# Adding the attention masks by a matrix product in place of a masked reduction

## The chip, the cores and the metric

The kernel runs on one core of a Trainium2 chip. The metric is the device time of one execution in microseconds (us); of several executions the median is given. A core has TensorE (PE in the rows, its weight loads as PEld), VectorE (DVE), ScalarE (ACT), GpSimd (POOL) and SyncE (SP), which run side by side and wait for each other by semaphores.

## The reference

One sequence of 256 positions with 1024 channels goes through four layers and their norms, all in 32-bit numbers: a layer of attention in a sliding window with a sink ("a", 16 heads), a layer of causal attention ("b", 16 heads), and two hybrid layers ("h", 8 heads each) with dilated attention, a state-space scan and a gated feed-forward part. Every attention has this core; the mask differs per kind:

```python
s = jnp.einsum('bnikgd,bnjkd->bnkgij', qb, kband).astype(jnp.float32) * scale
...
s = jnp.where(mask[None, :, None, None], s, NEG)
sink = jnp.broadcast_to(sinks.astype(jnp.float32).reshape(kvh, G)[None, None, :, :, None, None],
                        s.shape[:-1] + (1,))
p = jax.nn.softmax(jnp.concatenate([s, sink], axis=-1), axis=-1)[..., :-1]
o = jnp.einsum('bnkgij,bnjkd->bnikgd', p.astype(v.dtype), vband)
```

A softmax needs the greatest masked score of each row. A head has 64 channels, and scale is 1/8.

## The kernel before, in words

Nearly all work is projections: 512-column products of activations with weight chunks (L1000). A 32-bit weight chunk comes by DMA into `raw`; ScalarE rounds it to `hi` (L1161), VectorE takes the rest as `lo` (L901), each in two halves, and TensorE multiplies hi and lo parts, three products for one. There are three buffers of each, and a half is split two chunks ahead of its use (`due`).

Everything else is a list of steps that `build_schedule` writes down in one order; every engine walks through this list and issues its own part of each step, so the order on each engine is fixed by the list. `attention(sc, n)` places the attention of one pair of heads beside the projection chunks: first `pv` of the pair before last, then `flip` of the last pair, then `scores` of the new pair. Between two such calls stand the twelve products of half a chunk, and in some places more.

A 128-row query tile by its keys gives 128 columns for the first tile and 256 for the second; the 384 columns of a head (`QC`) lie side by side in one PSUM bank. A step `scores` does this for two heads:

- TensorE (L1040 to L1056) waits until both banks are free, and multiplies queries by keys, 64 rows deep, one head on rows 0 to 63, the other on rows 64 to 127 (L1052 for the first query tile, L1055 for the second).
- VectorE (L1639 to L1648), for each head and each of the two tiles, runs one `tensor_tensor_reduce`: it adds the mask to the scores, scales by -1/8, writes the result back into the bank, and puts the minimum (in "a" begun from the negated sink, else from `BIG`) into `shift`, one number per row and tile. The mask is in `masks`, bf16, three strips of 384 columns with 0 or -1e30. The profile shows each as two instructions of L1644.
- ScalarE (L1285 to L1295) takes the exponential of minus the bank plus `shift` into `prob` (L1293, L1294).

`flip` transposes `prob` (three products of 128 columns a head, L975), ScalarE copies the result out (L1301; in "h" VectorE multiplies, L1654), `pv` multiplies by the values (L1075 to L1077), and `oev` copies the output out of PSUM on ScalarE (L1308). Steps other than projections take PSUM banks 4 to 7 in turn; a bank is free when the last reader of its former content is done. `identb`, the identity in bf16, is made at the start for the `decay` steps of the scan, which add their own mask by products (L1129, L1132).

Of the kernel before, what the change touches and what calls it, by code (L numbers as in the profile page):

```python
# [26 lines left out]
ALU = mybir.AluOpType  # L27
ACT = mybir.ActivationFunctionType
AXX = mybir.AxisListType.X

S, D, P = 256, 1024, 128
# [1 line left out]
KD = D // P  # L33
HD = 64
NEG = -1e30
BIG = 3e38
EPS = 1e-5
SCALE = HD ** -0.5
FF = 2816
# [15 lines left out]
QC = 3 * P  # L55
# [637 lines left out]
def build(nc, t):  # L693
# [24 lines left out]
    def keep(name, shape, dt=F32):  # L718
        return at(name, shape, dt)[0]

    at.end = 0
    h = keep("h", [P, M, D])
# [8 lines left out]
    masks = keep("masks", [P, 3 * QC + P + 32], BF16)  # L731
    csum = keep("csum", [P, P], BF16)
    identb = keep("identb", [P, P], BF16)
# [10 lines left out]
    sinks = keep("sinks", [P, 2, 16])  # L744
    small = keep("small", [P, 2, 3, 16])
    taps = keep("taps", [P, 10 * NCT])
    convw = taps[:, 0:8 * NCT].rearrange("p (l t c) -> p l t c", l=2, t=4)
    convb = taps[:, 8 * NCT:10 * NCT].rearrange("p (l c) -> p l c", l=2)
    shift = keep("shift", [P, 16, M])
    esink = keep("esink", [P, 16, M])  # L750
    dens = keep("dens", [P, M, 8])
# [89 lines left out]
    psum = [nc.alloc_psum_tensor(f"bank{i}", [P, 512], F32) for i in range(8)]  # L841
# [27 lines left out]
    def freed(eng, bank):  # L869

        if bank.before is not None:
            step, who = bank.before.freed
            if step.kind == "flip":
                eng.wait_ge(sem["flip", who], step.n + 1)
            else:
                ended(eng, step, who)
        return psum[4 + bank.at]
# [95 lines left out]
    def _(pe):  # L973
# [4 lines left out]
        for s in sc.steps:  # L978
# [61 lines left out]
            elif s.kind == "scores":  # L1040
# [6 lines left out]
                ended(pe, a["tq"][hd // 4], "scalar")  # L1047
                bank = freed(pe, s.bank)
                both = (bank, freed(pe, s.pair.bank))
                q, k = B["qT"], B["kT"]  # L1050
                for r, bank in zip((0, 64), both):
                    nc.tensor.matmul(bank[:, 0:P], q[r:r + 64, hd // 2, 0:P], k[r:r + 64, kv, 0:P],  # L1052
                                     start=True, stop=True)
                for r, bank in zip((0, 64), both):
                    nc.tensor.matmul(bank[:, P:QC], q[r:r + 64, hd // 2, P:S], k[r:r + 64, kv, 0:S],  # L1055
                                     start=True, stop=True).then_inc(sem["scores", "tensor"], 1)  # L1056
            elif s.kind == "flip":
                a = s.att
                B = Hb if a["kind"] == "h" else A
# [91 lines left out]
    def _(act):  # L1151
# [12 lines left out]
        def done(ins, s):  # L1164
            ins.then_inc(sem[s.kind, "scalar"], 1)
# [23 lines left out]
        for s in sc.steps:  # L1189
# [95 lines left out]
            elif s.kind == "scores":  # L1285
# [3 lines left out]
                if s.i >= 2:  # L1289

                    act.wait_ge(sem["flip", "tensor"], s.i - 1)
                bank, pr = psum[4 + s.bank.at], B[f"prob{s.p % 2}"]
                nc.scalar.activation(pr[:, 0:P], bank[:, 0:P], ACT.Exp, scale=-1.0, bias=shift[:, hd, 0:1])  # L1293
                done(nc.scalar.activation(pr[:, P:QC], bank[:, P:QC], ACT.Exp, scale=-1.0,  # L1294
                                          bias=shift[:, hd, 1:2]), s)  # L1295
            elif s.kind == "flip" and s.att["kind"] != "h":
                act.wait_ge(sem["flip", "tensor"], s.i + 1)
# [159 lines left out]
    def _(dve):  # L1457
        tt, ts, stt = nc.vector.tensor_tensor, nc.vector.tensor_scalar, nc.vector.scalar_tensor_tensor

        def chained(ins):  # L1460
            link(dve, "vector", ins)
# [5 lines left out]
        def done(ins, s):  # L1467
            ins.then_inc(sem[s.kind, "vector"], 1)
# [70 lines left out]
        for s in sc.steps:  # L1539
# [99 lines left out]
            elif s.kind == "scores":  # L1639
                a, hd = s.att, s.head  # L1640
                dve.wait_ge(sem["scores", "tensor"], s.i + 1)
                bank, at_ = psum[4 + s.bank.at], {"a": 0, "b": 1, "h": 2}[a["kind"]] * QC
                for m, c in enumerate((slice(0, P), slice(P, QC))):
                    last = nc.vector.tensor_tensor_reduce(  # L1644
                        bank[:, c], bank[:, c], masks[:, at_ + c.start:at_ + c.stop], -SCALE,
                        sinks[:, 1, hd:hd + 1] if a["kind"] == "a" else BIG, ALU.add, ALU.min,
                        shift[:, hd, m:m + 1])
                done(last, s)  # L1648
            elif s.kind == "flip" and s.att["kind"] == "h":
                dve.wait_ge(sem["flip", "tensor"], s.i + 1)  # L1650
                if s.i >= 2:
# [163 lines left out]
```

## Time and profile before

| | us |
|---|---|
| median of 3 runs | 922.65 |
| lowest, highest | 921.39, 923.07 |
| profiled execution, its own time | 923.07 |
| its span in the trace | 921.2 |
| TensorE busy | 882.9 |
| VectorE busy | 558.5 |
| ScalarE busy | 518.6 |
| GpSimd busy | 127.7 |

The span runs from the first to the last instruction of the program; the execution's time lies around it. Busy times of engines overlap. A product's busy time includes its way through the array, so two products that follow each other overlap in the rows; their starts tell the pace.

### The profile page before, as it was taken

The numbers are of one execution on the slowest core, as the hardware profiler recorded it, in microseconds if no ns is written. First come the engines' busy times: TensorE is split into PE (matmuls) and PEld (weight loads), VectorE is DVE, ScalarE is ACT, GpSimd is POOL, SyncE is SP. The second block draws the span as 40 slices with busy tenths as digits, with TensorE's granted clock in tenths as the row PEclk, the third lists the DMA queues.
The fourth block names the chain that finished last, engine by engine and source line by source line (L and its number), as shares of the span: only waits on it lengthen the run. The fifth ranks groups of instructions, "written<-read, shape, count | busy, mean of one in ns | idle before, by whom it ended". The sixth has DMA issues, their size and how long they took to land.

```text
span 921.2 us, 12293 instructions
## 1 busy us (share of the span) xinstructions
PE 882.9 (96%) x4557; PEld 728.8 (79%) x4557; DVE 558.5 (61%) x969; ACT 518.6 (56%) x853; POOL 127.7 (14%) x103
## 2 busy tenths in 40 slices
PE   4899998999999999999999999999999999999995
PEld 3787887878787888788888888887888888888884
DVE  4754578546766567865555544756677755555443
ACT  3567755676487685464444433677874644444331
POOL 0031103421015350000000000042430000000000
PEclk9899999999999999999999999999999999999998
DMA  8641344443544424576565555534423766565521
GB/s 279 218 150 57 129 163 157 140 129 102 177 167 139 137 93 136 164 236 187 188 185 183 183 183 185 193 104 139 137 92 120 246 190 188 186 190 189 196 95 46
DMA packets 94846, 146.88 MB, mean 159 GB/s; under 512 B 6476, under 2 KB 54852, under 8 KB 94788
## 3 DMA queue, kind: packets, MB, share of 16 engines
q1 hardware_dynamic: 91392, 139.14, 46.3%
q0 software_dynamic: 1440, 5.24, 2.0%
q10 hardware_dynamic: 1956, 1.71, 0.5%
q8 instruction: 37, 0.61, 0.3%
q14 instruction: 21, 0.17, 0.1%
HBM read 145.04 MB, written 1.05 MB: 159 GB/s over the span
## 4 chain that ended last, share of the span: by engine, by line
PE 70%; issue 21%; DVE 3%; ACT 2%; DMA 2%; POOL 0%; ACTq 0%; POOLq 0%; DVEq 0%
PE bank L1000 55%; PE bank L975 6%; PE bank L1141 1%; PE bank L1052 1%; PE bank L1055 1%; PE bank L1077 1%; PE bank L1076 1%; DMA taps_stage<-in_conv_b 1%; PE bank L1075 1%; DMA gains<-in_norm_g 1%; ACT junk L1186 1%; DVE lo L901 1%; ACT hi L1161 1%; DVE hyb_MT L1749 1%; PE bank L1120 0%
## 5 line engine op out<-in xcount | busy, mean ns | idle before, releaser
L901 DVE TENSOR_TENSOR lo<-raw,hi 128x1024 fp32r<-128x1024 f32 x246 | 302.4, 1254 | 133.7 <-ACT hi L1161 131.6
L1161 ACT ACTIVATE hi<-raw 128x1024 fp32r<-128x1024 f32 x262 | 268.4, 1056 | 77.0 <-PE bank L1000 69.9
L1000 PE MATMUL bank<-hi,xT_hi 128*128 128x512 f32 (+2 forms) x736 | 294.4, 400 | 8.5 <-DVE lo L901 3.1
L1000 PE MATMUL bank<-hi,xT_lo 128*128 128x512 f32 (+2 forms) x736 | 285.5, 388 | 0.0
L1000 PE MATMUL bank<-lo,xT_hi 128*128 128x512 f32 (+2 forms) x736 | 284.5, 387 | 0.0
L1000 PEld LDWEIGHTS bank<-hi,xT_hi 128*128 128x128 f32 x736 | 140.0, 190 | 41.6 <-issue 13.8
L1000 PEld LDWEIGHTS bank<-hi,xT_lo 128*128 128x128 f32 x736 | 139.6, 190 | 28.9
L1000 PEld LDWEIGHTS bank<-lo,xT_hi 128*128 128x128 f32 x736 | 140.3, 191 | 25.5 <-issue 0.5
L1000 PE MATMUL bank<-hi,hT 128*128 128x512 f32 x352 | 111.2, 395 | 0.0
L1000 PEld LDWEIGHTS bank<-hi,hT 128*128 128x128 f32 x352 | 66.3, 188 | 15.4
L1000 PE MATMUL bank<-lo,hT 128*128 128x512 f32 x176 | 69.4, 395 | 0.0
L1000 PE MATMUL bank<-hi,oT_hi 128*128 128x512 f32 x160 | 66.9, 418 | 0.0
L1000 PE MATMUL bank<-hi,oT_lo 128*128 128x512 f32 x160 | 62.7, 392 | 0.0
L1000 PE MATMUL bank<-lo,oT_hi 128*128 128x512 f32 x160 | 62.4, 390 | 0.0
L1208 ACT ACTIVATE hT<-bank 128x512 fp32r<-128x512 f32 x22 | 13.2, 598 | 77.2 <-PE bank L975 77.2
L1577 DVE TENSOR_TENSOR hT<-bank,hT 128x512 fp32r<-128x512 f32 x22 | 15.2, 692 | 59.3 <-ACT hT L1208 59.3
L975 PE MATMUL bank<-cst,quarter 128*128 128x128 f32 x264 | 39.4, 277 | 12.0 <-DVE quarter L1571 10.1
L1258 ACT ACTIVATE silu_gate<-bank,rms 128x256 f32<-128x256 f32 x44 | 20.7, 475 | 50.3 <-PE bank L1000 50.3
L975 PEld LDWEIGHTS bank<-cst,quarter 128*128 128x128 f32 x264 | 32.8, 143 | 20.2 <-issue 10.3
L901 POOL TENSOR_TENSOR lo<-raw,hi 128x1024 fp32r<-128x1024 f32 x16 | 38.2, 2399 | 74.1 <-ACT hi L1161 74.1
L1612 DVE SCALAR_TENSOR_TENSOR quarter<-bank,rms,silu_gate 128x256 f32<-128x256 f32 x44 | 19.3, 479 | 41.1 <-ACT silu_gate L1258 41.1
L1736 DVE SCALAR_TENSOR_TENSOR hyb_acc<-bank,taps,hyb_acc 128x255 f32<-128x255 f32 (+2 forms) x72 | 29.2, 474 | 19.9 <-ACT hyb_acc L1333 19.9
(230 smaller groups left out, 983.5 us busy)
## 6 DMA issues: line engine op xcount, KB each, us to landing
raw<-in_w_in SPq DMA_DIRECT2D x26, 1024.0 KB, 5.1
raw<-in_w_gate SPq DMA_DIRECT2D x44, 512.0 KB, 4.0
raw<-in_w_up SPq DMA_DIRECT2D x44, 512.0 KB, 4.9
raw<-in_w_down SPq DMA_DIRECT2D x22, 1024.0 KB, 4.9
raw<-in_w_out SPq DMA_DIRECT2D x20, 1024.0 KB, 5.1
raw<-in_w_in_b SPq DMA_DIRECT2D x10, 1024.0 KB, 5.1
raw<-in_w_in_a SPq DMA_DIRECT2D x8, 1024.0 KB, 7.8
gains<-in_norm_g POOLq DMA_DIRECT2D x2, 512.0 KB, 6.8
```

The costliest lines, as they stand in the source:

```text
L901: return engine.tensor_tensor(lo[r][:, cols], raw[c.i % RAW][:, cols], hi[r][:, cols].bitcast(F32), ALU.subtract)
L975: return nc.tensor.transpose(out, in_, ident)
L1000: last = nc.tensor.matmul(bank[:, 0:wd], still[a], mv[r][:, off:off + wd], start=c.first and i == 0 and j == 0, stop=c.last and i == len(t ...
L1052: nc.tensor.matmul(bank[:, 0:P], q[r:r + 64, hd // 2, 0:P], k[r:r + 64, kv, 0:P], start=True, stop=True)
L1055: nc.tensor.matmul(bank[:, P:QC], q[r:r + 64, hd // 2, P:S], k[r:r + 64, kv, 0:S], start=True, stop=True).then_inc(sem["scores", "tensor"], 1)
L1075: nc.tensor.matmul(bank[:, c0:c0 + W1], pt[:, 0:P], v[:, 0, kv, :], start=True, stop=True)
L1161: nc.scalar.activation(hi[c.i % SPLIT][:, cols], raw[c.i % RAW][:, cols], ACT.Copy)\
L1208: done(nc.scalar.activation(out, bank[:, :], ACT.Copy), s)
L1258: last = nc.scalar.activation(sil[s.i % 2][:, m, :], bank[:, 0:UPW], ACT.Silu, scale=rms[:, 1, m:m + 1])
L1577: done(tt(b, bank[:, :], a.bitcast(F32), ALU.subtract), s)
L1612: last = stt(quarter[s.buf][:, m * UPW:(m + 1) * UPW], psum[2 * s.block["pair"] + m][:, UPW:2 * UPW], rms[:, 1, m:m + 1], sil[s.i % 2][:, ...
L1736: ins = stt(acc[:, tap:S], x[:, 0:S - tap], cw[:, 3 - tap, ct:ct + 1], acc[:, tap:S], ALU.mult, ALU.add)
```

## The change

The mask is put into the banks by TensorE: before the score products, and after the waits for the banks, each of the two banks gets one product of `identb` with the mask's strip of 384 columns, which starts the accumulation; the score products then add to it. VectorE takes the plain maximum of the 128 and the 256 columns into a new tile `rowmax` (L1647, L1648 of the changed kernel), waits for its own second maximum, and makes `shift` of both by one operation on 128x2 elements: times -1/8, in "a" also the minimum with the negated sink. The bank is not written by VectorE any more, and ScalarE's exponential uses the scale 1/8 in place of -1.

```diff
-BIG = 3e38
...
+    rowmax = keep("rowmax", [P, 2, 4])
...
                 both = (bank, freed(pe, s.pair.bank))
+                mk = {"a": 0, "b": 1, "h": 2}[a["kind"]]
+                for bank in both:
+                    nc.tensor.matmul(bank[:, 0:QC], identb[:, :], masks[:, mk * QC:(mk + 1) * QC],
+                                     start=True, stop=False)
                 q, k = B["qT"], B["kT"]
                 for r, bank in zip((0, 64), both):
                     nc.tensor.matmul(bank[:, 0:P], q[r:r + 64, hd // 2, 0:P], k[r:r + 64, kv, 0:P],
-                                     start=True, stop=True)
+                                     start=False, stop=False)
                 for r, bank in zip((0, 64), both):
                     nc.tensor.matmul(bank[:, P:QC], q[r:r + 64, hd // 2, P:S], k[r:r + 64, kv, 0:S],
-                                     start=True, stop=True).then_inc(sem["scores", "tensor"], 1)
+                                     start=False, stop=True).then_inc(sem["scores", "tensor"], 1)
...
-                nc.scalar.activation(pr[:, 0:P], bank[:, 0:P], ACT.Exp, scale=-1.0, bias=shift[:, hd, 0:1])
-                done(nc.scalar.activation(pr[:, P:QC], bank[:, P:QC], ACT.Exp, scale=-1.0,
+                nc.scalar.activation(pr[:, 0:P], bank[:, 0:P], ACT.Exp, scale=SCALE, bias=shift[:, hd, 0:1])
+                done(nc.scalar.activation(pr[:, P:QC], bank[:, P:QC], ACT.Exp, scale=SCALE,
                                           bias=shift[:, hd, 1:2]), s)
...
                 dve.wait_ge(sem["scores", "tensor"], s.i + 1)
-                bank, at_ = psum[4 + s.bank.at], {"a": 0, "b": 1, "h": 2}[a["kind"]] * QC
-                for m, c in enumerate((slice(0, P), slice(P, QC))):
-                    last = nc.vector.tensor_tensor_reduce(
-                        bank[:, c], bank[:, c], masks[:, at_ + c.start:at_ + c.stop], -SCALE,
-                        sinks[:, 1, hd:hd + 1] if a["kind"] == "a" else BIG, ALU.add, ALU.min,
-                        shift[:, hd, m:m + 1])
-                done(last, s)
+                rm = rowmax[:, s.i % 2, :]
+                nc.vector.tensor_reduce(rm[:, 0:1], psum[4 + s.bank.at][:, 0:P], AXX, ALU.max)
+                chained(nc.vector.tensor_reduce(rm[:, 1:2], psum[4 + s.bank.at][:, P:QC], AXX, ALU.max))
+                if a["kind"] == "a":
+                    done(ts(shift[:, hd, :], rm[:, 0:2], -SCALE, sinks[:, 1, hd:hd + 1], ALU.mult, ALU.min), s)
+                else:
+                    done(ts(shift[:, hd, :], rm[:, 0:2], -SCALE, None, ALU.mult), s)
```

On TensorE, at the first pair of heads of the first layer, stood before (an x2 is the pair's two heads; hi and lo are the weight parts, bank is a PSUM bank):

```order
L1000 MATMUL bank<-lo_61,xT_hi 128x512
L1000 MATMUL bank<-hi_58,xT_lo 128x512
L1052 MATMUL bank<-attn_kT,attn_qT 128x128 x2
L1055 MATMUL bank<-attn_kT,attn_qT 128x256 x2
L1000 MATMUL bank<-hi_59,xT_hi 128x512
L1000 MATMUL bank<-lo_62,xT_hi 128x512
```

and now:

```order
L1000 MATMUL bank<-lo_61,xT_hi 128x512
L1000 MATMUL bank<-hi_58,xT_lo 128x512
L1052 MATMUL bank<-masks,identb 128x384 x2
L1056 MATMUL bank<-attn_kT,attn_qT 128x128 x2
L1059 MATMUL bank<-attn_kT,attn_qT 128x256 x2
L1000 MATMUL bank<-hi_59,xT_hi 128x512
L1000 MATMUL bank<-lo_62,xT_hi 128x512
```

The row of `masks` is new, two products; the score products keep their place behind it, and nothing else of TensorE's order moves.

On VectorE, for the same pair, stood before (ISA is the masked reduction and, with 128x1, the read of its result; the waits are the ones for TensorE's scores and for ScalarE's half of a split):

```order
L901 TENSOR_TENSOR lo_60<-raw_54,hi_57 128x1024 [waits chunk_scalar] x2
L1644 ISA bank,shift<-bank,masks,sinks 128x128 [waits scores_tensor]
L1644 ISA shift 128x1
L1644 ISA bank,shift<-bank,masks,sinks 128x256
L1644 ISA shift 128x1
L1644 ISA bank,shift<-bank,masks,sinks 128x128 [waits scores_tensor]
L1644 ISA shift 128x1
L1644 ISA bank,shift<-bank,masks,sinks 128x256
L1644 ISA shift 128x1
L901 TENSOR_TENSOR lo_61<-raw_55,hi_58 128x1024 [waits chunk_scalar]
```

and now:

```order
L901 TENSOR_TENSOR lo_60<-raw_54,hi_57 128x1024 [waits chunk_scalar] x2
L1647 TENSOR_REDUCE rowmax<-bank 128x1 [waits scores_tensor]
L1648 TENSOR_REDUCE rowmax<-bank 128x1
L1650 TENSOR_SCALAR shift<-rowmax,sinks 128x2 [waits chain_vector]
L1647 TENSOR_REDUCE rowmax<-bank 128x1 [waits scores_tensor]
L1648 TENSOR_REDUCE rowmax<-bank 128x1
L1650 TENSOR_SCALAR shift<-rowmax,sinks 128x2 [waits chain_vector]
L901 TENSOR_TENSOR lo_61<-raw_55,hi_58 128x1024 [waits chunk_scalar]
```

Eight instructions of a pair became six; the last of each head waits for the one before it, and behind it in the queue stand the second head's maxima and the next split.

## Rows read from the trace of the kernel before

**Rows 1.** The page's busy times, and a stretch of attention: us, busy, ..., PEclk, DMA share, GB/s

```profile
PE 882.9 (96%) x4557; PEld 728.8 (79%) x4557; DVE 558.5 (61%) x969; ACT 518.6 (56%) x853; POOL 127.7 (14%) x103
...
50.00:110.00 60.00, 58.70 (x370) 48.33 (x370) 30.70 (x85) 44.19 (x85) 14.70 (x13) 1.00 0.30 100
```

**Rows 2.** Waits of TensorE: line <- releaser: us in total, times, longest

```profile
PE bank L1052 <- ACT hyb_o L1308: 2.7, 2, 1.4
PE bank L1052 <- ACT attn_o L1308: 2.5, 2, 1.3
```

**Rows 3.** L1052's records (ns), then timeline 52 to 60: start, us, engine, line [idle]

```profile
L1052 PE MATMUL bank<-attn_kT,attn_qT x64: 272/308/374, 53.8 to 208.9; 64*128 64x128 f32 x64
...
53.23 0.39 PE L1000 MATMUL bank<-lo,xT_hi 128*128 128x512 f32 x1
...
53.45 0.39 PE L1000 MATMUL bank<-hi,xT_lo 128*128 128x512 f32 x1
53.77 0.30 PEld L1052 LDWEIGHTS bank<-attn_kT,attn_qT 64*128 64x128 f32 x4 [0.35 <-issue]
...
56.53 0.47 ACT L1294 ACTIVATE attn_prob<-bank,shift 128x256 f32<-128x256 f32 x1
...
57.49 0.81 PE L975 MATMUL bank<-cst,attn_prob 128*128 128x128 f32 x6
...
58.24 0.30 PEld L1052 LDWEIGHTS bank<-attn_kT,attn_qT 64*128 64x128 f32 x4 [0.17 <-issue]
```

**Rows 4.** L1129's weight loads (ns), then the critical chain: start, us, what

```profile
L1129 PEld LDWEIGHTS bank<-masks,identb x64: 96/98/99, 327.9 to 696.9; 128*128 128x128 bf16 x64
...
328.09 0.06 PE bank L1132
...
328.92 0.06 PE bank L1132
```

**Rows 5.** VectorE's timeline at one pair of the first layer and one of the second

```profile
71.62 0.36 DVE L1644 CUSTOM_DVE_ANT_0 bank<-bank,masks,sinks 128x128 f32<-128x128 f32 x1 [2.16 <-PE bank L1055]
...
72.30 0.14 DVE L1644 DVE_READ_ACCUMULATOR2_ANT shift<- 128x1 f32 x1
...
72.98 0.14 DVE L1644 DVE_READ_ACCUMULATOR2_ANT shift<- 128x1 f32 x1
...
185.34 0.30 DVE L1644 CUSTOM_DVE_ANT_0 bank<-bank,masks 128x128 f32<-128x128 f32 x1 [2.28 <-PE bank L1055]
...
185.56 0.47 DVE L1644 CUSTOM_DVE_ANT_0 bank<-bank,masks 128x256 f32<-128x256 f32 x1
...
186.57 0.14 DVE L1644 DVE_READ_ACCUMULATOR2_ANT shift<- 128x1 f32 x1
```

**Rows 6.** VectorE's timeline at the chained Newton steps of the first norm

```profile
27.57 0.17 DVE L1597 TENSOR_SCALAR newt<-newt 128x2 f32<-128x2 f32 x1
27.78 0.16 DVE L1598 TENSOR_TENSOR rms<-rms,newt 128x2 f32<-128x2 f32 x1
27.86 2.35 DVE L901 TENSOR_TENSOR lo<-raw,hi 128x1024 fp32r<-128x1024 f32 x2
```

**Rows 7.** Timelines of ScalarE and TensorE before two waits for L1308

```profile
72.48 0.37 ACT L1293 ACTIVATE attn_prob<-bank,shift 128x128 f32<-128x128 f32 x1 [1.16 <-DVE shift L1644]
...
77.30 0.39 ACT L1308 ACTIVATE attn_o<-bank 128x260 f32<-128x260 f32 x1
...
77.84 0.49 PE L1052 MATMUL bank<-attn_kT,attn_qT 64*128 64x128 f32 x4 [1.30 <-ACT attn_o L1308]
...
288.44 0.37 ACT L1293 ACTIVATE hyb_prob<-bank,shift 128x128 f32<-128x128 f32 x1 [2.05 <-DVE shift L1644]
...
296.51 0.36 ACT L1308 ACTIVATE hyb_o<-bank 128x260 f32<-128x260 f32 x1
```

**Rows 8.** The page's group of VectorE's splits: busy us, mean ns, idle before

```profile
L901 DVE TENSOR_TENSOR lo<-raw,hi 128x1024 fp32r<-128x1024 f32 x246 | 302.4, 1254 | 133.7 <-ACT hi L1161 131.6
```

**Rows 9.** A group of VectorE by line: busy us, mean ns, idle before

```profile
L1749 DVE TENSOR_TENSOR hyb_MT<-hyb_E,hyb_cb 128x512 f32<-128x512 f32 x16 | 14.0, 887 | 4.0 <-ACT hyb_E L1366 4.0
```

## The prediction

> **What bounds the kernel now.** I read the page's busy times first, then the table of waits of TensorE, then the timeline around the score products, and last the timelines of VectorE and ScalarE there. TensorE is busy for 882.9 of 921.2 us [rows 1]; the chain that ended last runs mostly through it. So whatever is added to TensorE's stream is paid unless it falls into a wait, and whatever is taken from VectorE pays only where TensorE waits for it. The reader should see in the waits that TensorE's whole waiting at the score products is 2.7 + 2.5 = 5.2 us, at four places, and that there it waits for ScalarE (L1308, the copy of the attention output out of PSUM) [rows 2].
>
> There are 16 + 16 + 8 + 8 = 48 heads, taken two at a time, so 24 pairs. A product of 32-bit operands leaves two records; 64 records for the first two layers [rows 3] are 32 heads.
>
> **The added matrix products.** Each pair gets two products of the identity with a mask strip, bf16, 384 columns, all 128 rows of the array: 48 in all. None has this width in the trace. The nearest rows are L1129 and L1132, bf16 products of 128 columns, which follow each other in 0.06 us: from 328.09 to 328.92 there are 14 steps, 0.059 us each [rows 4]. Three times that is 0.177 us, an upper end, since whatever is fixed in a product is counted three times. The granted clock in attention is 1.00, the 2.4 GHz level [rows 1], so 0.059 us are 142 clocks for 128 columns; at exactly a clock a column 384 columns would take 0.160 us, the lower end. The 512-column products of the projections start 0.22 us apart (53.23, 53.45) [rows 3]; three quarters of that is 0.165 us, and I take that, as the nearest row in width: 48 x 0.165 = 7.9 us, with ends 48 x 0.160 = 7.7 and 48 x 0.177 = 8.5 us. The weight load of such a product takes 0.10 us [rows 4], and the 128-column products keep a step of 0.059 us although each has one, so it lies beside the product before it.
>
> Does the change of array shape cost anything new? The score products use half the rows (64*128). Their first weight load comes 0.32 us after the start of the last projection product (53.45 to 53.77), which another projection product would have followed after 0.22 us; and after the flips, whose six products step by 0.11 us, the last one starts at 57.49 + 0.81 - 0.27 = 58.03 and the load at 58.24, 0.21 us later [rows 3]. So entering the half-row shape costs about 0.10 us beyond the step of the product in front, whichever it is. With the change the mask product stands in front; the number of switches stays. It costs nothing more where TensorE runs without a wait. The Trainium skill (TensorEngine Tiling (Array Packing), Key Properties) says that changing the tiling mode drains the engine; the rows agree with about 0.10 us of it, and by that rule alone the sum would be the same, as the masks sit on the 128-row side of a switch that was there before.
>
> At the four places where TensorE waits before the scores, the 0.10 us used to pass inside the wait. Now the masks come after the wait (the wait is for the bank they write) and the switch after them: 4 x 0.10 = 0.4 us more.
>
> **VectorE's part of a pair.** Removed: 96 masked reductions and their 96 accumulator reads of 0.14 us, and the writing of the masked scores back into the bank. Added: 96 plain maxima, 48 waits of VectorE for its own maximum, and 48 operations on 128x2 elements. Before, a pair in the first layer took 1.50 us (71.62 to 72.98 + 0.14), and the first head's numbers were there at 72.30 + 0.14 = 72.44. In the later layers, where the limit is a constant, a pair took 1.37 us (185.34 to 186.57 + 0.14); there the second reduction starts 0.22 us after the first and takes 0.47 us [rows 5]. No plain maximum stands in the trace. It has one operand fewer and writes no strip back. If it costs what the masked one does, with the steps of the later layers, a head is 0.22 + 0.47 (the second must now end) + 0.03 + 0.17 = 0.89 us, and the next head starts some 0.09 us before that end: 0.80 + 0.89 = 1.69 us a pair against 1.37. The 0.03 us and the 0.17 us are read from the Newton steps, which are chained in the same way (27.57, 0.17 long, next at 27.78), and the 0.09 us from the unchained successor at 27.86 of the step at 27.78 [rows 6]. If it is 0.1 us shorter each, the pair takes about 1.4 us, as now. So the latency of the pair changes by 0 to +0.35 us, and I take +0.25, nearer the row of the same width and source, because the wait for the end is certain and the saving is not.
>
> Where does this lie on the path? At most pairs nowhere. After the scores of the first pair TensorE has twelve projection products; ScalarE's last exponential ends at 56.53 + 0.47 = 57.00 and the flips start at 57.49 [rows 3], the second head's 0.33 us later, so the head that is late has 0.8 us of slack; and the table of waits names no wait of a flip (L975) for ScalarE at any pair. VectorE's next split (L901) is queued behind the new wait, but VectorE stands idle before its splits for 131.6 us in all, waiting for ScalarE [rows 8]. But the four waits of 1.3 us are another matter: there ScalarE runs without a pause from the first exponential (72.48, which waited for VectorE) over the second head's, the split, a table load and the gate's silu to the copy L1308 at 77.30, and TensorE starts the next scores at 77.84 after 1.30 us of waiting. The same chain runs in the hybrid layers from 288.44 to 296.51 [rows 7]. What VectorE is late there, TensorE pays one to one: 4 x 0.25 = 1.0 us, ends 0 and 4 x 0.35 = 1.4 us.
>
> ScalarE's 96 exponentials keep their count and size; only a constant and what stands in the bank change: nothing. Memory traffic: none.
>
> **Sum.** 7.9 + 0.4 + 1.0 = 9.3 us on TensorE's path. The profiled execution took 923.07 us (span 921.2), so it would be 932.4; it lay 0.42 us above the median of 922.65, so the median becomes 932.0 us (+1.0%). Ends: 7.7 + 0.4 + 0 = 8.1 and 8.5 + 0.4 + 1.4 = 10.3 us, that is 930.7 and 933.0.
>
> **Rivals.**
> (1) *Slow maxima.* VectorE could take far longer over a plain maximum. The dearest row per column is L1749, 887 ns for 512 columns, 1.73 ns a column [rows 9]; at that rate, with the 0.17 us of a 128x2 operation as fixed part, the two of a head take 0.39 and 0.61 us, the second starting 0.31 us after the first; a head takes 0.31 + 0.61 + 0.20 = 1.12 us, a pair 2.15 us, +0.8. On the four chains this is 3.2 us, and two or three tight pairs begin to wait (0.4 us together): 7.9 + 0.4 + 3.2 + 0.4 = 11.9 us, 934.6. Against it: the masked reduction of 256 columns takes 0.47 us, two operands and all. Chance 0.08. The Trainium skill (VectorE: DVE Perf Modes, Rules for kernel authors) calls tensor_reduce the slowest VectorE operation and advises to restructure; it speaks against this change, and no row here shows a reduction of that kind.
> (2) *Masks that do not stream.* If every mask product must be out of the array before what follows it (the first for the change of number type, the second because it follows one), each costs 0.165 + 0.10 us: 48 x 0.265 = 12.7, and with 0.4 + 1.0 us as above 14.1 us, 936.8. For it: 0.10 us is what a switch does cost here. Against it: L1132 adds into the columns that L1129 has just written at a step of 0.059 us. Chance 0.06.
> (3) *Cheap all round.* Masks at a clock a column, and maxima so short that the first exponential starts 0.3 us earlier and the four waits shrink by as much: 7.7 + 0.4 - 1.2 = 6.9 us, 929.6. Chance 0.08.
> (4) *Faster.* If a mask product were bound by issue and not by its columns, it would cost the 0.06 us of L1129: 2.8 us. If VectorE's stage then shrank by over 1 us a pair, the waits before the scores, 5.2 us, would go: 2.8 - 5.2 = -2.4 us, 920.3. It decides below (5.2 - 1.8) / 48 = 0.07 us a mask, and only with all four waits gone. Against it: TensorE's steps follow the columns (0.059 us for 128, 0.22 for 512), and the new VectorE stage has one more dependent step. Chance 0.02; with half of it, no change, 0.02.
>
> **How the numbers follow.** Forecast 0.74, (1) 0.08, (2) 0.06, (3) 0.08, (4) 0.02, no change 0.02. A measurement of this kernel can tell about 0.2% (1.8 us) from none. Slower by more than that: 0.74 + 0.08 + 0.06 + 0.08 = 0.96; same 0.02; faster 0.02. The range takes in the forecast's ends and some 1 us on either side for the spread of the runs (921.39 to 923.07 before), up to the edges of (3) and (1): 929.8 to 934.2.
>
> **What the changed profile should show.** 48 more bf16 products before the half-row ones, 0.16 to 0.18 us apart; TensorE's busy time up by about 8 us; from the last 512-column product to the first score weight load 0.22 + 0.165 + 0.165 + 0.10 = 0.65 us in place of 0.32. The maxima with their 128x2 step should take 1.6 to 1.8 us a pair in place of 1.37 to 1.50, and the four waits before the scores should grow from 5.2 to about 6.2 us. Outside attention nothing moves. I am wrong if the masks step by under 0.1 us or over 0.2 us, if those waits shrink, or if the flips begin to wait for ScalarE.

## The result, and the profile after

The changed kernel takes 933.76 us (median of 4 runs, 932.42 to 935.81), the kernel before, measured beside it, 922.02 us (4 runs, 920.93 to 923.07). The ratio is 1.0137, with an interval from 1.0116 to 1.0158: slower by 11.7 us, where 9.3 us were forecast. The upper end of the forecast's range, 934.2, lies 11.55 us above the 922.65 us it was worked out from; the distance measured here is just beyond it. The profiled execution took 933.77 us, its span is 932.0 us.

The page of the changed kernel, busy times, against 882.9 us of TensorE before [rows 1]:

```profile
PE 891.8 (96%) x4605; PEld 731.1 (78%) x4605; DVE 565.8 (61%) x921; ACT 520.2 (56%) x853; POOL 127.4 (14%) x103
```

TensorE's table of waits in the changed kernel (line that waited, engine and line it waited for, us in total, times, longest), cut to the rows that answer to [rows 2] or are new:

```profile
PE bank L1052 <- ACT hyb_o L1312: 3.1, 2, 1.6
PE bank L1052 <- ACT attn_o L1312: 2.9, 2, 1.5
...
PE bank L1087 <- DVE hyb_probT L1658: 1.0, 1, 1.0
...
PE bank L1052 <- DVE hyb_acc L1740: 0.2, 1, 0.2
```

The four waits grew from 5.2 to 6.0 us, as forecast (6.2). Two waits are new: 1.0 us before L1087, the sums of the scan in the first hybrid layer, and 0.2 us before the masks of a later pair there.

The new instructions, from the views of the lines L1052, L1647, L1648, L1650 and L1652 (duration in ns as least, median and greatest; then first and last start in us; then the shape):

```profile
L1052 PE MATMUL bank<-masks,identb x48: 322/323/337, 51.6 to 643.3; 128*128 128x384 bf16 x48
```

```profile
L1647 DVE TENSOR_REDUCE rowmax<-bank x48: 274/285/293, 53.0 to 645.3; 128x1 f32<-128x128 f32 x48
```

```profile
L1648 DVE TENSOR_REDUCE rowmax<-bank x48: 406/414/418, 53.2 to 645.5; 128x1 f32<-128x256 f32 x48
```

```profile
L1650 DVE TENSOR_SCALAR shift<-rowmax,sinks x16: 228/229/810, 53.6 to 98.7; 128x2 f32<-128x2 f32 x16
```

```profile
L1652 DVE TENSOR_SCALAR shift<-rowmax x32: 168/169/821, 170.8 to 645.9; 128x2 f32<-128x2 f32 x32
```

The plain maximum of 256 columns takes 0.41 us, less than the masked one of 0.47 [rows 5], and nowhere near the 0.61 of rival (1). What stands out is the third column of the last two rows: the operation on 128x2 elements sometimes takes 0.8 us in place of 0.17.

TensorE's timeline at the first two pairs of the first layer (start and duration in us; an x2 or x4 is a run of products under its first start):

```profile
51.37 0.39 PE L1000 MATMUL bank<-hi,xT_lo 128*128 128x512 f32 x1
51.60 0.50 PE L1052 MATMUL bank<-masks,identb 128*128 128x384 bf16 x2
52.03 0.49 PE L1056 MATMUL bank<-attn_kT,attn_qT 64*128 64x128 f32 x4
```

```profile
55.74 0.82 PE L975 MATMUL bank<-cst,attn_prob 128*128 128x128 f32 x6
56.39 0.49 PE L1052 MATMUL bank<-masks,identb 128*128 128x384 bf16 x2
```

The last projection product starts at 51.37, the masks at 51.60, the scores at 52.03: 0.66 us in place of the 0.32 of [rows 3], and 0.65 was forecast. The masks step by 0.165 us (the x2 runs 0.50 us, one product 0.32 to 0.34) and the switch of shape takes the rest of the 0.43 us. Behind the flips of the second pair, whose last starts at 55.74 + 0.82 - 0.27 = 56.29, the masks come 0.10 to 0.11 us later, which is the flips' own step.

At the third pair this is no longer so. The timelines of TensorE and ScalarE in the changed kernel:

```profile
61.84 0.82 PE L975 MATMUL bank<-cst,attn_prob 128*128 128x128 f32 x6
62.58 0.48 PE L1052 MATMUL bank<-masks,identb 128*128 128x384 bf16 x2
```

```profile
62.04 0.39 ACT L1312 ACTIVATE attn_o<-bank 128x260 f32<-128x260 f32 x1 [0.61 <-PE bank L1081]
```

and the same place in the kernel before:

```profile
63.28 0.82 PE L975 MATMUL bank<-cst,attn_prob 128*128 128x128 f32 x6
64.03 0.49 PE L1052 MATMUL bank<-attn_kT,attn_qT 64*128 64x128 f32 x4
```

```profile
63.48 0.39 ACT L1308 ACTIVATE attn_o<-bank 128x260 f32<-128x260 f32 x1 [0.53 <-PE bank L1077]
```

In both, ScalarE's copy of the output out of PSUM, which frees one of the two banks, ends while the flips still run, at 62.04 + 0.39 = 62.43 and at 63.87, and TensorE starts in the bank 0.15 and 0.16 us after that. Before, this lay inside the 0.20 us that lead from the last flip to a half-row product anyway: at the second pair, where no bank is waited for, it is 0.20 us too [rows 3]. Now the masks could follow the last flip after 0.11 us, and come after 0.19 (62.39 to 62.58). At 0.08 us such a gap is too short to be a wait in the table. The place with a long wait shows the same 0.14 us between the end of the copy, 76.83 + 0.39 = 77.22, and the masks:

```profile
76.83 0.39 ACT L1312 ACTIVATE attn_o<-bank 128x260 f32<-128x260 f32 x1
```

```profile
77.36 0.48 PE L1052 MATMUL bank<-masks,identb 128*128 128x384 bf16 x2 [1.53 <-ACT attn_o L1312]
```

VectorE's part of the first pair in the changed kernel:

```profile
52.98 0.29 DVE L1647 TENSOR_REDUCE rowmax<-bank 128x1 f32<-128x128 f32 x1 [1.14 <-PE bank L1059]
53.19 0.41 DVE L1648 TENSOR_REDUCE rowmax<-bank 128x1 f32<-128x256 f32 x1
53.64 0.29 DVE L1650 TENSOR_SCALAR shift<-rowmax,sinks 128x2 f32<-128x2 f32 x1
...
54.48 0.23 DVE L1650 TENSOR_SCALAR shift<-rowmax,sinks 128x2 f32<-128x2 f32 x1
```

From 52.98 to 54.71 it takes 1.73 us (1.50 before [rows 5]), in the later layers about 1.55 (1.37 before).

The new wait of 1.0 us has its cause some microseconds ahead of it. VectorE, GpSimd and TensorE in the changed kernel, three views of the same stretch:

```profile
280.90 2.50 DVE L1713 TENSOR_TENSOR hyb_da<-hyb_dt,small 128x48 f32<-128x48 f32 x2
283.33 1.01 DVE L1658 TENSOR_TENSOR hyb_probT<-bank,cst 128x384 f32<-128x384 f32 x2
```

```profile
280.98 4.69 POOL L901 TENSOR_TENSOR lo<-raw,hi 128x1024 fp32r<-128x1024 f32 x2 [5.04 <-ACT hi L1165]
```

```profile
284.02 0.38 PE L1087 MATMUL bank<-hyb_da,cst 128*128 128x32 f32 x2 [0.96 <-DVE hyb_probT L1658]
```

and VectorE and GpSimd in the kernel before:

```profile
276.18 0.33 DVE L1709 TENSOR_TENSOR hyb_da<-hyb_dt,small 128x48 f32<-128x48 f32 x2
```

```profile
276.30 4.80 POOL L901 TENSOR_TENSOR lo<-raw,hi 128x1024 fp32r<-128x1024 f32 x2 [4.86 <-ACT hi L1161]
```

Two small operations of VectorE, which write `hyb_da`, took 0.33 us before and take 2.50 us now. Nothing in them changed. Before, GpSimd started a split 0.12 us after the first of the two, which is just when the second started, and neither was held; now it starts 0.08 us after the first, and the second operation, 0.04 us later than GpSimd, ends only when GpSimd's first half (4.69 / 2 = 2.35 us) is over. `hyb_probT`, queued behind it, is late, and so are the sums on TensorE. The second hybrid layer shows the same collision (the pair of operations takes 2.53 us at 619.73), but there `hyb_probT` had waited 1.98 us for TensorE's flips before, which covers it.

### The profile page after: what moved, and what is told of

Same layout as the page of the kernel before. It is cut to its first block, busy times and chain, and to the rows that moved or that the text cites. A ratio compares the mean times of both kernels' runs of the same rounds, so it can differ in the third digit from the quotient of the medians.

```text
span 932.0 us, 12341 instructions
## 1 busy us (share of the span) xinstructions
PE 891.8 (96%) x4605; PEld 731.1 (78%) x4605; DVE 565.8 (61%) x921; ACT 520.2 (56%) x853; POOL 127.4 (14%) x103
## 4 chain that ended last, share of the span: by engine, by line
PE 66%; issue 21%; DVE 6%; ACT 4%; DMA 2%; POOL 0%; ACTq 0%; POOLq 0%; DVEq 0%
PE bank L1000 51%; PE bank L975 6%; DVE lo L901 1%; PE bank L1145 1%; PE bank L1059 1%; DMA taps_stage<-in_conv_b 1%; PE bank L1056 1%; PE bank L1081 1%; PE bank L1080 1%; ACT hi L1165 1%; PE bank L1052 1%; ACT junk L1190 1%; PE bank L1079 1%; DMA gains<-in_norm_g 1%; DVE hyb_MT L1753 1%
## 5 line engine op out<-in xcount | busy, mean ns | idle before, releaser
L975 PE MATMUL bank<-cst,quarter 128*128 128x128 f32 x264 | 39.4, 277 | 11.7 <-DVE quarter L1575 9.8
```

The costliest lines, as they stand in the source:

```text
L975: return nc.tensor.transpose(out, in_, ident)
```

## The experiments

The median of the kernel before was 921.26 us in the first group of runs, 919.93 in the second and 919.99 in the third; each ratio is against the one of its own group. "Step" below is what one pair of heads adds on TensorE's path: how much further the first projection product behind its scores has moved against the kernel before, since the same point of the pair ahead. Steps leave out what lies ahead of the first pair, where the change does nothing: there the profiled execution of the kernel before, at a granted clock of 0.93 in its first 51 us, was 2.8 us later than that of the repeated change, at 0.97.

**The change once more**, beside the others of the first group, the kernel unaltered.

> The changed kernel once more, on the same chip as the parts: 11 to 12 us over before. The sum of the parts is 9 + 1 = 10 by theory F, and more than the parts if the arrival and the longer VectorE stage collide only together.

Measured: 931.82 us, ratio 1.0115 (1.0096 to 1.0133). The steps add up to 11.3 us: 0.32 or 0.33 at most of the pairs that open a layer (two each), 0.36 to 0.42 at most others, 0.59 at the four waited ones, 1.31 at the pair with the late sums. That is more than the medians differ by (10.6 us) and less than in the first measurement (11.7).

**Masks by product alone.** The products are added, VectorE keeps its masked reduction (so the mask is in the scores twice).

```diff
 # before.py
+                for bank in both:
+                    nc.tensor.matmul(bank[:, 0:QC], identb[:, :], masks[:, mk * QC:(mk + 1) * QC],
+                                     start=True, stop=False)
```

> The 48 mask products alone: TensorE adds the masks ahead of the score products, VectorE keeps the masked reduction of before (it adds the mask a second time, which changes no exponential). Theory F, the working of the forecast: 48 x 0.165 + 4 x 0.10 = 8.3 us over before, and nothing else. Theory H, that hidden waits come to light: the waits for the banks at some ten pairs, which lay inside the 0.10 us of the array switch, now cost 0.07 us each before the masks, so 9.0 to 9.3 us, and the step from the last flip product to the first mask is 0.18 us at those pairs in place of 0.11. Theory V, that VectorE's new chain is the larger cause: under 8.3 us here.

Measured: 930.44 us, 1.0102 (1.0083 to 1.0122): 9.2 us of the loss. The waits stay what they were before (compare [rows 2]), and the one at the sums is not there:

```profile
PE bank L1053 <- ACT hyb_o L1312: 2.8, 2, 1.4
...
PE bank L1053 <- ACT attn_o L1312: 2.5, 2, 1.3
```

The steps are 0.32 where the banks are long free, and 0.37 to 0.44, mostly 0.41, both at the four waited pairs and at the others behind the second of a layer, with one exception: 0.21 at the third pair of the first hybrid layer. So 0.08 to 0.09 us a pair beyond the two products comes from TensorE alone, and at fifteen pairs, not at four. At the exception the bank came free by a copy of VectorE (`hyb_acc`), and TensorE had already lost 0.2 us to it before. The time alone does not decide between the forecast's 8.3 us and the 9.0 to 9.3 us of exposed waits, as the interval reaches from 7.6 to 11.2 us; the steps do, and the way from the last flip to the first mask: 0.18 us at twelve pairs of this trace with nothing of VectorE's part changed, against 0.11 us where the banks are long free.

**Maxima alone.** The plain maxima without the products; the masks are left out of the computation, and the score products start the accumulation again, as before.

```diff
 # after.py
-                for bank in both:
-                    nc.tensor.matmul(bank[:, 0:QC], identb[:, :], masks[:, mk * QC:(mk + 1) * QC],
-                                     start=True, stop=False)
```

> VectorE's and ScalarE's part of the change alone; the masks are left out of the scores. Theory F: 4 x 0.2 us through the four waits before the scores, about 1 us over before. Theory V: 2 to 3 us, because GpSimd holds up some of the 48 new operations on 128x2 elements (0.8 us in place of 0.17) and TensorE waits once for VectorE in the first hybrid layer (1.0 us). If the collision in the hybrid layer comes from TensorE's later arrival and not from the maxima, it is not here.

Measured: 923.61 us, 1.0036 (1.0012 to 1.0060), 2.35 us of the loss. With the 9.2 above this makes 11.5, against 10.6 for the whole change beside them, which agrees within the intervals. The 2.35 is loose: no execution took near 923.6 us, five took 921 and five 926 to 930 (last section). The wait at the sums is there without any mask product, and longer:

```profile
275.20 0.38 PE L1083 MATMUL bank<-hyb_da,cst 128*128 128x32 f32 x2 [1.63 <-DVE hyb_probT L1654]
```

**Masks twice.** The masks-alone kernel with a second pair of products behind the first (the mask is in the scores three times).

```diff
 # the kernel with masks by product alone
+                for bank in both:
+                    nc.tensor.matmul(bank[:, 0:QC], identb[:, :], masks[:, mk * QC:(mk + 1) * QC],
+                                     start=False, stop=False)
```

> As the masks alone, but every mask is added twice, 96 products. If a mask product costs its step on TensorE's path, this lies 48 x 0.165 = 7.9 us above the masks alone, whatever the waits do; if masks drain (0.265 each) 12.7 us; if the excess of the masks alone over 8.3 us is a one-time cost of arriving later it does not double.

Measured: 936.52 us, 1.0165 (1.0145 to 1.0185). TensorE's timeline:

```profile
50.70 0.50 PE L1053 MATMUL bank<-masks,identb 128*128 128x384 bf16 x2
51.03 0.49 PE L1056 MATMUL bank<-masks,identb 128*128 128x384 bf16 x2
```

The second two start 0.33 us after the first two, 0.165 us each: they stream, even where one adds into columns just written. The steps are 0.65 and 0.72 us, so the second pair of products adds 0.28 to 0.35, and 24 x 0.32 = 7.7 us in all. The medians differ by 6.1 us; the masks-alone executions had the lower granted clock, 0.992 to 0.995 in the mean of an execution against 0.994 to 0.996, which goes the right way but was not separated. Rival (2), masks that must leave the array one by one, is out: each would add 0.265.

**Masks behind the scores.** The scores begin the accumulation and the masks end it.

```diff
 # after.py
-                for bank in both:
-                    ... (mask product, start=True) ahead of the scores
+                for bank in both:
+                    nc.tensor.matmul(bank[:, 0:QC], identb[:, :], masks[:, mk * QC:(mk + 1) * QC],
+                                     start=False, stop=True).then_inc(sem["scores", "tensor"], 1)
```

> The change with the mask products behind the score products instead of ahead of them (same 48 products, VectorE as changed). The masks alone stepped TensorE later by 0.32 us at pairs where the banks were long free and by 0.41 us at the others, where a wait of 0.07 to 0.10 us used to pass inside the switch of array shape. Theory H, exposed waits: with the switch ahead of the masks again, every pair costs 0.32 to 0.34 us, so this is 16 x 0.09 = 1.4 us under the change. Theory S, that the extra is a property of the mask product (its weight load after the flips): no difference to the change, within 0.3 us.

Measured: 930.68 us, 1.0109 (1.0085 to 1.0134). TensorE's timeline at the first pair:

```profile
51.50 0.49 PE L1052 MATMUL bank<-attn_kT,attn_qT 64*128 64x128 f32 x4
...
52.36 0.50 PE L1059 MATMUL bank<-masks,identb 128*128 128x384 bf16 x2
52.56 0.53 PE L1000 MATMUL bank<-hi,xT_hi 128*128 128x512 f32 x1
```

The step falls to 0.20 to 0.25 at most pairs, below the 0.32 to 0.34 that was expected from exposed waits alone. Two things went. The difference between pairs with and without a bank that is just free is gone: the half-row products are first again, and the bank is awaited inside their switch. And the two masks put the next product back by 0.20 us only (52.36 to 52.56), not by 0.33: this was not expected, and its cause is not shown. The first mask comes 0.31 us behind the last half-row product, as the projection product did before, and the projection product is recorded only 0.03 us behind the second mask. The four waited pairs keep more (0.39 to 0.45 at three of them), and the wait at the sums stays at 0.9 us. By the steps this version is some 2 us ahead of the change; the times show no difference (1.0109 against 1.0115).

**Row maxima in PSUM.** `rowmax` is four columns of the bank in place of a tile in SBUF.

```diff
 # after.py
-                rm = rowmax[:, s.i % 2, :]
+                rm = psum[4 + s.bank.at][:, QC:QC + 4]
```

> The change with the two maxima of a head kept in the free columns 384 to 387 of the scores' own bank, so that the operation that makes shift reads PSUM and not SBUF. Theory G, that GpSimd holds up VectorE where it reads SBUF alone: no such operation takes over 0.3 us (0.8 us before, at the pairs beside GpSimd's gates and splits). For the time: nothing or up to 0.3 us less, as these pairs have slack; the 1.0 us wait in the first hybrid layer stays.

Measured: 933.84 us, 1.0145 (1.0120 to 1.0169). The changed kernel, VectorE at 91.68 and GpSimd beside it:

```profile
91.68 0.75 DVE L1650 TENSOR_SCALAR shift<-rowmax,sinks 128x2 f32<-128x2 f32 x1
```

```profile
91.36 1.04 POOL L1435 TENSOR_TENSOR quarter<-attn_o,dens 128x512 f32<-128x512 f32 x1
```

and VectorE at the same place with the maxima in PSUM, and there all of L1652:

```profile
91.73 0.22 DVE L1650 TENSOR_SCALAR shift<-bank,sinks 128x2 f32<-128x2 f32 x1
```

```profile
L1652 DVE TENSOR_SCALAR shift<-bank x32: 158/159/163, 170.8 to 644.0; 128x2 f32<-128x2 f32 x32
```

GpSimd no longer holds the operation up, at any pair. Time is not gained: these places have slack, and the wait at the sums stays at 1.0 us. So the held-up `shift` is real, but costs only what two late pairs shrink by: the last pair of the first layer from a step of 0.52 to 0.38, the third of the first hybrid layer from 0.54 to 0.23.

**A late VectorE in the kernel before.** One small chained operation more on VectorE, ahead of the chain that ends in `hyb_da`, and nothing of the change.

```diff
 # before.py
+                chained(nc.vector.memset(rowmax[:, 0, :], 0.0))
                 ended(dve, s.before, "scalar")
```

> The kernel before with one more VectorE operation (a memset of four columns and a wait for it, some 0.15 to 0.2 us) ahead of the softplus chain of each hybrid layer, behind the first pair's scores. Theory A, arrival: in the kernel before, the last two operations of that chain (hyb_da) ended 0.1 us after GpSimd began its split; as late as this they are held for about 2 us, and TensorE waits about 1 us in the first hybrid layer at the sums. Theory N, that the maxima themselves cause it: no such wait, and the time is that of before within 0.3 us.

Measured: 930.15 us, 1.0095 (1.0061 to 1.0128). From the table of waits, the VectorE groups, and the timelines of VectorE and GpSimd:

```profile
PE bank L1084 <- DVE hyb_probT L1655: 5.8, 2, 3.7
```

```profile
L1711 DVE TENSOR_TENSOR hyb_da<-hyb_dt,small 128x48 f32<-128x48 f32 x4 | 9.3, 2365 | 0.1
```

```profile
275.84 4.63 DVE L1711 TENSOR_TENSOR hyb_da<-hyb_dt,small 128x48 f32<-128x48 f32 x2
```

```profile
275.76 4.65 POOL L902 TENSOR_TENSOR lo<-raw,hi 128x1024 fp32r<-128x1024 f32 x2 [4.85 <-ACT hi L1162]
```

Without a mask product and without a plain maximum, a fraction of a microsecond on VectorE puts GpSimd's start ahead of the first `hyb_da` (275.76, 275.84), the two operations are held through one half of the split each (4.63 us beside 4.65), in both hybrid layers (four operations, 2365 ns each, where they took 204), and TensorE waits 5.8 us at the sums. It is arrival that decides. The waits are not all of the 10.2 us: at the two pairs of the first hybrid layer around the 3.7 us wait TensorE falls back by 6.4 us, and the granted clock there is 0.53 from 280 to 285 us and 0.79 from 285 to 290. The kernel before stands at the edge of this. The change goes over it by one operation of the two, and pays in the layer where nothing covers it.

**The pair's scores in front of, or behind, the chain.** In the changed kernel the last step of the chain (`soft`, 3) goes ahead of the attention step beside it.

```diff
 # after.py
-do(turn_keys, sc, a, kr) + do(soft, 2), att(0) + do(soft, 3)
+do(turn_keys, sc, a, kr) + do(soft, 2), do(soft, 3) + att(0)
```

> The change with VectorE's softplus chain ahead of the first pair's maxima in each hybrid layer. Theory A: the chain is through before GpSimd's split starts, hyb_da takes 0.3 us again, TensorE's wait of 0.95 us at the sums is gone, and the time is 1 us under the change. If the chain has to wait for ScalarE instead, the first pair's maxima are late and the flips of the first pair wait.

Measured: 939.15 us, 1.0204 (1.0180 to 1.0227), the slowest of all. From the groups and from TensorE's timeline:

```profile
L1713 DVE TENSOR_TENSOR hyb_da<-hyb_dt,small 128x48 f32<-128x48 f32 x4 | 0.7, 204 | 0.1
```

```profile
297.78 0.48 PE L1052 MATMUL bank<-masks,identb 128*128 128x384 bf16 x2 [1.86 <-DVE hyb_acc L1740]
```

The collision is gone and with it the wait at the sums, which was expected. But the attention of the pair is late by the length of the chain, and a wait of 1.9 us, with one of 1.6 us in the second hybrid layer, stands before later masks. That was not expected: I had followed one chain and not the one that takes its place. The two pairs with these waits have steps of 2.5 and 2.1 us, against 0.55 and 0.40 in the repeated change; another 1.2 us each stand at the third pair of the first layer and at the first of the second, which this edit does not touch.

**Taking the four waits away.** In the kernel before and in the changed one, the gate's silu (and its like in the hybrid layers) is put behind the attention step, so that ScalarE copies the output first.

```diff
 # both kernels
-    za = evacs(sc, b, "ev_z", j=0, kind_of=which)
     sc.goes_on(att(4))
+    za = evacs(sc, b, "ev_z", j=0, kind_of=which)
...
-do(conv_silu, 0) + att(3)
+att(3) + do(conv_silu, 0)
```

> The kernel before with ScalarE's order changed at the four places where TensorE waits before the scores: the gate's silu (ev_z) of layers a and b, and the first conv_silu of the hybrid layers, stand behind the attention step instead of ahead of it, so the copy L1308 that frees the bank no longer waits for a table load and two to four silus. Theory: the four waits of 1.2 to 1.4 us before the scores go, 5 us under before. If the silus only move the wait (to the next projection's bank or to a later flip), within 1 us of before.

> The changed kernel with the same order. If VectorE's longer stage reaches TensorE only through those four waits and the one at the sums, the distance to the kernel before with the same order is about 0.8 us smaller than that of the change to the kernel before: 10 us or a little more in place of 11.

Measured: 922.81 us, 1.0018 (1.0000 to 1.0036), and 931.62 us, 1.0120 (1.0094 to 1.0145). TensorE's timeline of the kernel before in the new order:

```profile
83.57 0.49 PE L1052 MATMUL bank<-attn_kT,attn_qT 64*128 64x128 f32 x4 [1.34 <-ACT attn_o L1308]
```

The wait of 1.30 us at 77.84 [rows 7] is gone, and one of 1.34 us stands at the next pair; in the hybrid layers likewise one of 1.38 us comes later, at the next transposes. ScalarE has the same work to do between two points; in whatever order it does it, the bank after it is late. My expectation of 5 us for the kernel before falls. For the changed one I had expected the distance between the two to be 0.8 us smaller than without the new order. Their medians differ by 8.8 us, but by the steps of the two traces it is 11.0 against 11.3 us: the four pairs step by 0.34 to 0.39 in place of 0.59, and two of the pairs behind them by 0.58 and 0.60 in place of 0.36 and 0.39. That part of the cost moves with the wait.

**All of it together**: masks behind the scores, maxima in PSUM, and the new order.

> The changed kernel with everything that the runs so far point to: masks behind the scores (0.22 to 0.25 us a pair in place of 0.32 to 0.41), maxima in the bank's free columns, and the new order. 3 us under the change in the new order, and still 6 to 8 us over the kernel before in the new order: what is left are 24 x 0.23 = 5.5 us of mask products and the wait at the sums.

Measured: 933.22 us, 1.0128 (1.0104 to 1.0153), no better than the change itself, 1.6 us above the changed kernel in the new order where 3 us below was expected, and 10.4 us above the kernel before in that order where 6 to 8 were. Away from the moved waits the steps are the small ones of the masks behind the scores (0.20 to 0.30), but the wait at the sums is still 1.0 us, and after the moved waits the clock falls, as its row for the stretch 85 to 90 us shows (the last three numbers: granted clock, share of the DMA engines, GB/s):

```profile
85.00:90.00 5.00, 4.95 (x20) 3.63 (x21) 2.77 (x10) 3.85 (x9) 0.00 (x0) 0.66 0.00 0
```

No version tried is faster than the kernel before.

## Why the prediction was wrong by some 2 us

The direction was right, and so were the three terms that the forecast had; two costs stood at nothing that are real. The size was short by 2.4 us against this measurement, and by 1.3 us against the second one, which lies inside the forecast's range. Term by term, what the steps of the repeated change show:

| term | forecast, us | shown, us |
|---|---|---|
| mask products | 7.9 | 24 x 0.33 = 7.9 |
| switch no longer inside the four waits | 0.4 | 4 x 0.08 = 0.3 |
| VectorE through the four ScalarE chains | 1.0 | 4 x 0.18 = 0.7 |
| "It costs nothing more where TensorE runs without a wait" | 0 | 12 pairs, 0.03 to 0.22 each: 1.0 |
| "Outside attention nothing moves" | 0 | 1.0 at the sums |
| first pairs of the second and of the last layer | 0 | 0.4 |
| sum | 9.3 | 11.3 |

- *Mask products.* Right: 0.165 us each, as the 512-column row scaled to 384 columns gave it. Alone and doubled they gave 0.32 to 0.33 a pair.
- *The switch inside the waits.* Right at the four places it was counted for. The failed step is the sentence behind it. I took the 0.20 us between the last flip and the first score weight load at one pair [rows 3] as the price of the switch at all pairs. At that pair it is; at eleven others the same 0.20 us also covered a wait for a bank, which the table of waits cannot show because it was never the later of the two. Putting a full-row product in front of the switch uncovered it. The masks-alone kernel shows this without VectorE's part, and the masks behind the scores show it gone. Not all of the 1.0 us is this: ten of the twelve pairs make up 0.6 us, and the other two (the last of the first layer, 0.15, and the third of the first hybrid layer, 0.22) are those that shrink when GpSimd no longer holds `shift` up.
- *VectorE's pair.* 1.55 us in the later layers against 1.37, +0.18, where +0.25 was taken: the second maximum is 0.05 us shorter than the masked one. The four waits went to 6.0 us for the forecast 6.2. Mechanism and place right, size a little high.
- *Outside attention.* Wrong, by 1.0 us, and the step that failed was to look for VectorE's lateness only on its way through ScalarE to the next scores. VectorE's own queue behind the pair held a chain whose last two operations stood right at the start of a GpSimd split; 0.04 us decided whether the second was held. The maxima alone bring the wait, the masks alone do not, and a small delay in the kernel before brings it several times over. That GpSimd stretches small operations was to be read in the trace of the kernel before, where 32 columns took 1.17 us beside it, and 0.19 us at the least:

```profile
147.03 1.35 POOL L1420 TENSOR_TENSOR attn_q<-attn_pool_rot,attn_pool_rot 128x512 f32<-128x512 f32 x1
147.26 1.17 DVE L1525 SCALAR_TENSOR_TENSOR trig_stage<-trig_stage,trig_stage 128x32 f32<-128x32 f32 x1
```

- *The rest.* 0.2 us each at the first pair of the second layer and of the last. The step there holds the passage from one layer to the next and differs between executions; the masks alone do not show the second (0.35 us). It was not separated further.
- *Rivals.* (1), slow maxima, gave 934.6 us, nearest to the result, for a reason that is not there: 0.41 us, not 0.61. That is a warning: the time alone would have seemed to prove it. Its rate was misread too: the 887 ns of L1749 [rows 9] are a mean over 16 of which four ran beside GpSimd and took 1.4 to 1.5 us; the median is 0.69 us, 1.35 ns a column. (2) is out by the doubled masks, (3) and (4) by the steps. The Trainium skill (VectorE: DVE Perf Modes, Rules for kernel authors) advises against the reduction as the slowest operation of VectorE. Here it took 0.41 us for 256 columns where the masked two-operand reduction took 0.47, so this trace does not agree.

What the table does not hold is spread from execution to execution, 929.0 to 933.3 us in the repeated change. The trace of the change shows one source: the granted clock in two stretches, from the wait of 1.57 us on that stands before the fourth pair of the first hybrid layer, at 303.9 us:

```profile
303.00:306.00 3.00, 2.07 (x11) 1.13 (x11) 0.16 (x2) 2.07 (x4) 0.00 (x0) 0.75 0.76 287
306.00:310.00 4.00, 4.00 (x16) 3.22 (x17) 1.41 (x6) 2.40 (x5) 0.73 (x1) 0.76 0.00 0
```

and in the repeated change, with the same wait of 1.54 us one microsecond earlier:

```profile
303.00:306.00 3.00, 3.00 (x18) 2.06 (x17) 1.48 (x6) 1.92 (x4) 0.00 (x0) 1.00 0.48 182
306.00:310.00 4.00, 4.00 (x21) 3.29 (x20) 1.46 (x4) 3.32 (x6) 2.39 (x1) 1.00 0.00 0
```

The fall costs about 1.6 us: the steps of this pair and the next are 1.25 and 1.51 us in the one trace, 0.61 and 0.55 in the other. That is more than the two measurements of the same kernel differ by (11.7 and 10.6 us). Why a wait of the same length brings it in one execution and not in the other stays open.

## What to carry to other kernels

A gap before an instruction is the greatest of several times, and a profile shows one of them: before putting work in front of a switch, a table load or a drain, look for what else ends within that gap, above all a buffer that comes free. When VectorE's stage gets longer by a tenth of a microsecond, follow its own queue as far as the next place where it runs beside GpSimd, not only the engines that wait for the stage. And a wait that comes from an amount of work between two points is not removed by another order of it; it stands at the next pair.

## What the runs showed of the hardware

- **GpSimd holds a small VectorE operation up for the whole of its own.** A 128x48 product of two SBUF operands takes 0.2 us alone; where GpSimd's 128x1024 half began 0.04 us or more ahead of it, it ends with that half, after 2.3 to 2.4 us; a 128x2 operation from SBUF goes from 0.17 to 0.8 us. The same operation with its source in PSUM keeps 0.16 us, and `hyb_probT`, which reads PSUM and one SBUF operand, its 0.5 us. The Trainium skill (SBUF — State Buffer, SBUF: two separate sides) describes a port pair of the two engines as an exclusive lock that goes to whoever starts first, for its whole instruction, and names a VectorE operation with two SBUF inputs against a GpSimd one that reads SBUF as such a case. These traces agree. Where GpSimd is recorded less than 0.01 us ahead of the second `hyb_da`, as in the kernel before, that operation is not held; where it is 0.04 us ahead or more, it is, so 0.04 us of arrival decides over 2 us.
- **A bf16 product of 384 columns steps by 0.165 us**, as its columns say, also when the next adds into the same bank. Ahead of half-row products two of them cost 0.32 to 0.33 us, behind them 0.20 to 0.25.
- **A bank is used 0.14 to 0.15 us after the copy that frees it has ended**, in the changed kernel, at waits of 0.07 and of 1.5 us alike.
- **The granted clock can fall after waits of 1.5 us, or not.** Maxima alone is the plainest: five executions at a mean granted clock of 0.996 to 0.997 took 920.8 to 921.4 us, five at 0.987 to 0.991 took 925.8 to 929.8 us, with one program. No trace of the slower five shows where theirs fell.
